# The sum of squares of the second half of the tokens is taken at the first k step of three projections instead of after the fourth

## What is computed

```python
def _rmsnorm(x, g):
    return x * lax.rsqrt(jnp.mean(x * x, axis=-1, keepdims=True) + 1e-6) * g

# first block, layer i (0: differential attention, 1: latent attention)
h = _rmsnorm(x, norm_g[i]) * (1.0 + scale) + shift
y = attention_i(h @ w_in...) @ w_out_i
x = x + gate * y
# end of the first block, start of the second
x = _rmsnorm(x, final_norm_g)
h = _rmsnorm(x, g_mix) * (1.0 + scale1) + shift1
y = mix(h @ w_in_2) @ w_out_2
x = x + (1.0 + gate1) * y
h = _rmsnorm(x, g_ffn) * (1.0 + scale2) + shift2
up = conv(h @ w_up)                      # then w_down, the last norm, the output
```

## Times and profile before

| | us |
|---|---|
| median of 3 runs | 3069.7 |
| lowest and highest | 3064.05 and 3071.18 |
| the execution that was profiled | 3066.07 |
| its span, from the first to the last instruction | 3064.3 |
| TensorE busy | 2789.9 (91%) |
| VectorE busy | 1686.1 (55%) |
| ScalarE busy | 1317.2 (43%) |
| mean granted clock of TensorE | 0.957 |

### The profile page before, as it was taken

How to read it: one execution, slowest core, us unless ns; L and a number is a source line. 1 busy time by engine, 2 the same in 40 slices (tenths; PEclk the granted TensorE clock), 3 DMA queues, 4 the chain that set the end, 5 groups by cost and what they waited for, 6 DMA issues and landing times.

```text
span 3064.3 us, 35100 instructions
## 1 busy us (share of the span) xinstructions
PE 2789.9 (91%) x13113; PEld 2184.1 (71%) x13113; DVE 1686.1 (55%) x2236; ACT 1317.2 (43%) x1878; POOL 0.2 (0%) x4
## 2 busy tenths in 40 slices
PE   4899999997899988998989789989799999999997
PEld 2677777775677766766777667666577878888775
DVE  5688888887453055555554635653754434334344
ACT  4566766665333133333333435655424323122232
POOL 0000000000000000000000000000000000000000
PEclk7999999998899999999999899999799999999998
DMA  7211111110211112121211310000211111111111
GB/s 259 98 35 48 48 48 41 48 34 27 89 35 45 50 40 64 50 68 50 68 55 56 105 42 28 22 15 14 90 41 42 47 49 46 50 48 41 51 39 68
DMA packets 216114, 168.08 MB, mean 55 GB/s; under 512 B 9594, under 2 KB 203090, under 8 KB 216018
## 3 DMA queue, kind: packets, MB, share of 16 engines
q1 hardware_dynamic: 215818, 166.73, 17.4%
q10 hardware_dynamic: 200, 0.06, 0.0%
HBM read 153.66 MB, written 13.11 MB: 54 GB/s over the span
## 4 chain that ended last, share of the span: by engine, by line
PE 79%; DVE 8%; ACT 5%; DVEq 3%; issue 2%; SPq 1%; DMA 1%; ACTq 0%
PE PS L518 19%; PE PS L520 18%; PE PS L519 18%; PE PS L1223 4%; PE PS L1870 3%; PE PS L1196 2%; PE PS L1210 2%; PE PS L1200 1%; PE PS L1825 1%; PE PS L1860 1%; PE PS L2334 1%; PE PS L2347 1%; DVEq L2012 1%; PE PS L2358 1%; DVE rest L509 1%
## 5 line engine op out<-in xcount | busy, mean ns | idle before, releaser
L518 PE MATMUL PS<-h_high,w_high 128*128 128x512 f32 x2096 | 843.1, 402 | 67.3 <-DVE h_low L952 24.1
L519 PE MATMUL PS<-h_low,w_high 128*128 128x512 f32 x2096 | 826.1, 394 | 0.0
L520 PE MATMUL PS<-h_high,w_low 128*128 128x512 f32 x2096 | 826.0, 394 | 0.0
L518 PEld LDWEIGHTS PS<-h_high,w_high 128*128 128x128 f32 x2096 | 400.2, 191 | 167.1 <-issue 55.5
L520 PEld LDWEIGHTS PS<-h_high,w_low 128*128 128x128 f32 x2096 | 399.2, 190 | 86.2
L519 PEld LDWEIGHTS PS<-h_low,w_high 128*128 128x128 f32 x2096 | 400.3, 191 | 80.6 <-issue 1.5
L540 DVE TENSOR_TENSOR w_low<-raw_weights,w_high 128x1024 fp32r<-128x1024 f32 (+2 forms) x156 | 179.4, 1153 | 212.6 <-ACT w_high L535 211.9
L535 ACT ACTIVATE w_high<-raw_weights 128x1024 fp32r<-128x1024 f32 (+2 forms) x156 | 155.7, 999 | 233.6 <-PE PS L520 223.9
L1299 ACT ACTIVATE residual<-PS,rest 128x1024 f32<-128x1024 f32 x128 | 141.5, 1111 | 174.2 <-DVE rest L1428 174.2
L2890 DVE SCALAR_TENSOR_TENSOR gated<-rest,gated 128x1024 f32<-128x1024 f32 x44 | 56.5, 1285 | 250.8 <-ACT gated L2858 250.8
L810 DVE SCALAR_TENSOR_TENSOR residual<-PS,rest,residual 128x512 f32 (+1 forms) x106 | 78.6, 749 | 197.8 <-PE PS L520 190.9
(11 more groups left out here) (333 smaller groups left out, 4114.4 us busy)
## 6 DMA issues: line engine op xcount, KB each, us to landing
raw_weights<-in_w_in SPq DMA_DIRECT2D x59, 512.0 KB, 4.1
activations<-in_w_ada SPq DMA_DIRECT2D x16, 1536.0 KB, 7.0
raw_weights<-in_w_up SPq DMA_DIRECT2D x44, 512.0 KB, 3.8
raw_weights<-in_w_out SPq DMA_DIRECT2D x24, 512.0 KB, 4.2
rest<-in_ada_w SPq DMA_DIRECT2D x16, 576.0 KB, 5.0
activations<-in_ada_w SPq DMA_DIRECT2D x8, 1024.0 KB, 14.2
x_kept<-residual SPq DMA_DIRECT2D x2, 4096.0 KB, 12.6
residual<-x_kept SPq DMA_DIRECT2D x2, 4096.0 KB, 13.7
```

The costliest lines, as they stand in the source:

```text
L518: e.matmul(out_, wh[:, k, :], xh[:, k, cols], start=first, stop=False)
L519: e.matmul(out_, wh[:, k, :], xl[:, k, cols], start=False, stop=False)
L520: return e.matmul(out_, wl[:, k, :], xh[:, k, cols], start=False, stop=last_k)
```

## The change

In the two places that are not fused (`norm1`, `norm4`) TensorE does the sum of the second half after k step 0 of the next projection, not after k step 3; ScalarE and VectorE keep their order. In the fused place (`norm3`) TensorE does the two matmuls of the sum ahead of step 0, ScalarE takes the first root of the second half after tile 0 (it was tile 3) and the second root after tile 3 (it was 5), and VectorE does `middle` of the second half after its step t = 2 (it was 4). No instruction is added or removed.

```diff
@@ NormHalves.scalar
                 self.second_rstd(e, 0)
             for t in range(NT):
                 self.high(e, 0, t)
-                if t == 3:
+                if t == (0 if self.fused else 3):
                     self.rstd(e, 1)
-                if t == 5 and self.fused:
+                if t == 3 and self.fused:
                     self.second_rstd(e, 1)
@@ NormHalves.vector
                 if t == 1 and not self.fused:
                     self.add(e, 1)
-                if t == 4 and self.fused:
+                if t == 2 and self.fused:
                     self.middle(e, 1)
@@ pe_two_tiles
+        if halves.fused:
+            halves.stat_pe(e, 1)
         for h in range(2):
             for k in range(NT):
                 ...
-                if h == 0 and k == 3:
+                if h == 0 and k == 0 and not halves.fused:
                     halves.stat_pe(e, 1)
```

## The result

| | before | after |
|---|---|---|
| median | 3065.47 us (5 runs) | 3049.23 us (5 runs) |
| lowest and highest | 3064.05 and 3071.18 | 3044.12 and 3052.52 |
| profiled execution, its span | 3064.3 | 3042.5 |

The ratio is 0.9934 with a 95% interval of 0.9922 to 0.9946: 16.5 to 23.9 us faster, 20.2 in the middle. The two medians of the table differ by 16.2 us, those of the two later timings by 21.7 each. The forecast gain was 15.6 us, with bounds of 8.8 and 17.6. The forecast time, 3054.1 us, started from 3069.7, the median of three runs; the five runs have 3065.47.

A forecast was written before the change was run, and what follows sets the result against it. TensorE bounds the kernel (79% of the chain), waiting for tile 4 behind the second half's sum. Gains 5.1 + 4.2 + 6.3 = 15.6 us from 3069.7 give 3054.1 us; range 3046 to 3061.7, gain bounds 8.8 to 17.6.

The forecast's parts named there:

- bounds of 8.8 and 17.6: Whole kernel: lowest and highest gain in us, from 2.9 to 5.5 (first), 2.9 to 4.6 (last), 3.0 to 7.5 (fused).
- The loop of waits: All three places: TensorE's steps 1 to 3 hold up the root, the root tile 4, tile 4 TensorE; 2.87 us idle first.
- The terms: Gains forecast per stage: first place 5.1 us, fused place 6.3 us, last place 4.2 us.
- the bounds of 1.73 and 3.35: Fused place: the sum ahead of step 0 takes 1.73 us at full clock, 3.35 at half, hidden in TensorE's idle time.
- where I had 0.5: Fused place: the first root behind tile 0 delays VectorE's `low` of tile 1 by 0.5 us, unseen by TensorE.
- A: All three stages: a half-clock stretch of 1.6 us stays in each; gain 10.8 us, 3058.9 us; chance 0.20.
- B: Fused place gives 3.0 us instead of 6.3, for root and multiplications among first tiles; 12.3 in all; chance 0.09.
- C: Gain given back at the next unmoved wait, or a sum waits after all; 3069.7 us, give or take 3; chance 0.07.
- D: Work behind 905 shifts against clock changes; more half-clock stretches lose 26 us, giving 3080 us; chance 0.04.
- a fifth more: In D: 16 further half-clock stretches of 1.6 us loss each, on top of some 80 of 3.2 us.
- all of it moves along: End of first stage: the waits of ScalarE, VectorE and TensorE there move along with the 5.1 us gain.
- the end moves from 1721.05 by the same: Fused place: VectorE's rhythm rules before and after, so the stage's end comes 6.3 us earlier.

The follow-up runs named there:

- the two later timings: The changed kernel, unaltered, timed twice more against the kernel before: ratios 0.9938 and 0.9935.
- pe_only: Changed kernel with ScalarE's roots and VectorE's multiplications of the fused place back at their old places, TensorE's sum still early: 0.9951 of the kernel before.
- plain_k2: Changed kernel with the sum of the first and last place behind step 2 instead of step 0: 3057.87 us, one run.
- best_again: The file of pe_only_3 run again, unaltered, beside the changed kernel: 0.9942 of the kernel before, median 3049.6 us.
- the third job: The changed kernel, unaltered, timed a third time, beside best_again: 0.9935 of the kernel before, median 3046.1 us.
- before: The kernel before, without the change: median 3065.47 us in the first timing.
- after_again: The changed kernel once more, unaltered: 0.9938 of the kernel before, 19.0 us faster.
- pe_only_3: pe_only plus three small ScalarE activations at the end of the fused stage: 0.9914 of the kernel before, median 3041.4 us.
- delay_3: Kernel before plus three one-column ScalarE activations ahead of its split of the next weights, at the fused stage's end: 0.9985 of the kernel before.
- delay_8: Kernel before plus eight one-column ScalarE activations ahead of its split of the next weights, at the fused stage's end: 3065.33 us, one run.

## Where the prediction was right and where it was wrong

**The loop of waits.** Right, in all three places: with the sum early, ScalarE's root follows on tile 3 (or 0) with waits of 0.58, 0.24 and 0 us, and TensorE's waits for tile 4 are gone. `pe_only` (fused place) and `plain_k2` (the other two) show that it is the sum's place that counts.

**The terms.** 5.1, 6.3 and 4.2 us were forecast, 4.98, 6.22 and 4.13 measured, and two further profiles of the changed kernel give the stages again (27.12 and 27.11, 32.56 and 32.76, 27.10 and 27.10). In the first place the clock had fallen earlier than assumed, within step 0, and the sum has 1.84 us in its row; the root came 0.58 us late for that. In the fused place it took 2.58 us where I had 2.05 worked out between the bounds of 1.73 and 3.35, and tile 1 was held up by 0.65 us where I had 0.5. In the last place the end follows on TensorE before and after, and the term was off by 0.1 us.

**Rivals.** A, the half-clock stretches behind the resumption stay: no. In the first stage the granted clock is 0.94 where it was 0.89. In the windows of the kernel after, the clock is 1.00 in the whole last stage:

```profile
1674.67:1707.43 32.76, 28.19 (x99) 19.19 (x100) 28.58 (x41) 16.42 (x25) 0.00 (x0) 0.90 0.53 179
...
2255.00:2282.08 27.08, 23.77 (x96) 17.36 (x97) 23.80 (x36) 14.54 (x21) 0.00 (x0) 1.00 0.00 0
```

Before, it was 0.95 there, and in the fused stage 0.87 where it is 0.90 now. In the last stage TensorE waits about a tenth of a microsecond a step in VectorE's rhythm, and the clock holds. The Trainium skill (TensorE: Matmul & The Clock Gate, section "A second HAM failure mode: psum-queue depth-cycling") tells of a kernel whose clock went up and down with short idle times between groups of matmuls; this trace, at 1.00 over 27.08 us, does not agree. B, the fused place gives little: no, 6.2 us; its mechanism is there, but it costs 0.5 to 0.7 us and not 3.3. C, given back later: no; what lies behind each stage moved along with it. D, slower: no; and its count was wrong. In the kernel before 263 us run at half clock, as worked out (264), but in 36 stretches, the longest of 41 us (from 2144.4), and not in some 80 of 3.2 us. So "a fifth more" stood for nothing that the trace has.

**The step that failed** is what the sum leaves out. The prediction says of the work behind the first stage that "all of it moves along", of the fused one that "the end moves from 1721.05 by the same", and adds up 5.1 + 4.2 + 6.3 = 15.6 us with nothing for the work behind; its upper bound, 17.6, has no such term either. So the 20.2, 19.0 and 19.9 us of the three timings lie above that bound (their intervals reach below it, down to 14.4). Behind the fused place the same instructions took 3.9 to 4.1 us less, in all three profiles of the changed kernel, because TensorE ran them at half clock for 58 to 61 us instead of 72. Rival D had the means, the half-clock stretches that fall elsewhere when the work is displaced, but I gave it only one sign, a loss, and thought of it as chance for each run. It came as a gain, and it repeated in these three profiles, though `pe_only` and `best_again` show that an early sum alone does not secure it. With it the forecast would have been 15.6 + 4.0 = 19.6 us, which is what was measured (20.2, 19.0 and, in the third job, 19.9, each within some 4 us). A bound of some 4 us on both sides would have covered it; that is my estimate, from the 4 to 5 us over which the other unchanged stretches spread. I see nothing in the profile of before that gives its sign.

**What stays open.** The profiles part by when the clock falls just behind the fused stage, but not why. In `before` (long) and `after_again` (short) ScalarE's activations start within 0.1 us of each other, counted from the stage's end, up to some 235 us behind it; only then do the half-clock stretches fall elsewhere. How a fall 0.2 us earlier decides this was not tested, nor can it be said beforehand which version will meet which: `pe_only_3` and `best_again` are one file. Why this stretch takes lengths that repeat to a few tenths, while the ones ahead and between scatter by several microseconds, isn't settled either. Where the scatter of whole runs comes from was not tried by itself; in the five runs of the kernel after, times of 3044.1 to 3052.5 us go with granted clocks of 0.963 down to 0.959.

## To carry to other kernels

In this kernel, and likely in others like it, a reduction that another engine's next work waits for belongs into the first gap of TensorE in which its input is ready, ahead of matmuls that need nothing of it; find the gap by the time of its input, not by the place of its result. Move only what is late: in the fused place the moved matmuls did it all, and moving their followers up as well cost half a microsecond. And where TensorE's clock goes up and down, a change of some microseconds can also change how the work behind it meets the half-clock stretches; look for that share by cutting two traces at the same points, and take a delay of a fraction of a microsecond as the control, in more than one profile.

## What the runs showed of the hardware

- An added delay made a kernel faster: three activations of one column, 0.3 us, took 3.9 us off the 551.7 us behind them, with TensorE busy for 5.7 us less over the same matmuls. The same delay in `pe_only` gave 547.84 us behind the stage in one profile and 551.52 in another.
- The 551.6 us and the 547.7 us go with one sign: the granted clock falls 3.3 to 3.6 us behind the end of the stage, or 1.9 to 3.1 us.
- The clock held 1.00 over 27.08 us in which TensorE waited about 0.1 us in every 1.50.
- The kernel before against itself differed in its 23 runs of one job from 3058.7 to 3077.9 us, and one file gave medians of 3041.4 and 3049.6 us in two jobs. Differences under some 5 us can't be told from whole times; in the stages they mostly can: the first six profiles repeat each other's to 0.2 us. In unchanged stages `delay_3` had 31.63 us (32.2) in the first and 30.99 (31.2) in the last, `delay_8` 32.12 in the last, so up to 0.9 off.
- The partition sum of two matmul groups took 1.88 us by its rows at full clock, 3.35 and 3.54 where it was granted half clock for most of its time (mean clock 0.56 and 0.53), and 2.58 where the clock fell in its midst.
